# Attention heads: the swapped halves of q and k by transfers on ScalarE's queue, projections four units ahead, the output weights of the last head split earlier

## The reference

```python
def apply_rope(x, cos, sin):                       # x [B,T,H,2,64]
    x1, x2 = jnp.split(x, 2, -1)
    return jnp.concatenate([x1 * cos - x2 * sin, x2 * cos + x1 * sin], -1)

def diff_attention(...):                           # 8 heads, two maps of width 64 in each
    q, k, v = jnp.split(x @ w_in, 3, axis=-1)
    q, k = apply_rope(q, cos, sin), apply_rope(k, cos, sin)
    s = q k^T * 64 ** -0.5, causal                 # per head and map
    p = softmax(s)[map 0] - lam * softmax(s)[map 1]
    o = rms_norm(p @ v, subln_w) * (1.0 - lambda_init)
    return o @ w_out
```

## Time and profile before

| What | us |
|---|---|
| Median of 3 runs (1439.88 to 1441.41) | 1441.07 |
| The profiled execution's own time | 1440.98 |
| Its span, from first to last instruction | 1439.2 |
| TensorE busy | 1398.7 (97%) |
| VectorE busy | 868.1 (60%) |
| ScalarE busy | 649.8 (45%) |
| Attention's first `scores(0)` to its last head's | 860.18 to 1009.51 |
| Mean of the seven heads between them | 21.33 |

### The profile page before, as it was taken

The page is one execution under the profiler, slowest core; times in us unless marked ns, Lnnn a source line. Parts: engine busy times, 40 slices in busy tenths (PEclk is TensorE's granted clock), DMA queues, the critical chain, the costliest instruction groups (busy, mean ns, idle before and its releaser), DMA issues.

```text
span 1439.2 us, 20166 instructions
## 1 busy us (share of the span) xinstructions
PE 1398.7 (97%) x7042; PEld 1141.6 (79%) x7042; DVE 868.1 (60%) x1361; ACT 649.8 (45%) x1042; POOL 79.8 (6%) x92
## 2 busy tenths in 40 slices
PE   8799999999999999999999999999999999999997
PEld 7688888788788888888887876667688888888886
DVE  4566776666666666666524637777686666665226
ACT  4665666666433444444312235665524444443211
POOL 3000000000000000000001111111000000000002
PEclk9999999999999999999999999999999999999999
DMA  6122111121112333334322132121222333334331
GB/s 189 54 67 66 45 51 50 51 66 59 60 44 60 111 93 100 91 100 137 123 96 95 59 88 60 43 74 58 74 74 73 103 88 102 94 105 140 100 102 60
DMA packets 157727, 118.84 MB, mean 83 GB/s; under 512 B 5899, under 2 KB 145645, under 8 KB 157677
## 3 DMA queue, kind: packets, MB, share of 16 engines
q1 hardware_dynamic: 157676, 118.17, 27.4%
HBM read 116.04 MB, written 2.11 MB: 82 GB/s over the span
## 4 chain that ended last, share of the span: by engine, by line
PE 87%; DVE 8%; ACT 2%; issue 1%; DMA 1%; POOL 0%; SPq 0%; DVEq 0%; ACTq 0%
PE bank L1613 16%; PE bank L1615 16%; PE bank L1614 16%; PE bank L1601 8%; PE bank L1603 8%; PE bank L1602 8%; PE bank L1672 3%; PE bank L1679 2%; PE bank L1987 1%; PE bank L2005 1%; PE bank L1670 1%; PE bank L1948 1%; DVE w_lo L361 1%; PE bank L1579 1%; DVE Tc L1137 1%
## 5 line engine op out<-in xcount | busy, mean ns | idle before, releaser
L1613 PE MATMUL bank<-x_hi,w_hi 128*128 128x512 f32 (+1 forms) x1160 | 459.8, 396 | 3.6 <-DVE x_lo L1026 2.6
L1615 PE MATMUL bank<-x_hi,w_lo 128*128 128x512 f32 (+1 forms) x1160 | 438.3, 378 | 0.0
L1614 PE MATMUL bank<-x_lo,w_hi 128*128 128x512 f32 (+1 forms) x1160 | 437.7, 377 | 0.0
L361 DVE TENSOR_TENSOR w_lo<-raw,w_hi 128x1024 fp32r<-128x1024 f32 x194 | 237.9, 1229 | 243.8 <-ACT w_hi L356 238.4
L356 ACT ACTIVATE w_hi<-raw 128x1024 fp32r<-128x1024 f32 x186 | 195.0, 1051 | 168.9 <-PE bank L1603 139.6
L1613 PEld LDWEIGHTS bank<-x_hi,w_hi 128*128 128x128 f32 x1160 | 219.6, 189 | 42.0 <-issue 4.2
L1615 PEld LDWEIGHTS bank<-x_hi,w_lo 128*128 128x128 f32 x1160 | 218.9, 189 | 41.1
L1614 PEld LDWEIGHTS bank<-x_lo,w_hi 128*128 128x128 f32 x1160 | 219.7, 189 | 36.1 <-issue 2.9
L1601 PE MATMUL bank<-w_hi,u_hi 128*128 128x512 f32 x416 | 164.8, 396 | 3.0 <-DVE w_lo L361 3.0
L1603 PE MATMUL bank<-w_hi,u_lo 128*128 128x512 f32 x416 | 162.5, 391 | 0.0
L1602 PE MATMUL bank<-w_lo,u_hi 128*128 128x512 f32 x416 | 162.4, 390 | 0.0
(11 more groups left out here) (292 smaller groups left out, 1787.3 us busy)
## 6 DMA issues: line engine op xcount, KB each, us to landing
raw<-in_ffn_w_up SPq DMA_DIRECT2D x88, 512.0 KB, 3.8
raw<-in_ffn_w_down SPq DMA_DIRECT2D x44, 512.0 KB, 3.2
raw<-in_gdn_w_in SPq DMA_DIRECT2D x32, 512.0 KB, 4.1
raw<-in_diff_w_in SPq DMA_DIRECT2D x24, 512.0 KB, 3.7
raw<-in_gdn_w_out SPq DMA_DIRECT2D x8, 512.0 KB, 3.4
raw<-in_diff_w_out SPq DMA_DIRECT2D x8, 512.0 KB, 3.3
x_tok<-in_x SPq DMA_DIRECT2D x4, 512.0 KB, 5.9
ROW<-decay_rows SPq DMA_DIRECT2D x8, 256.0 KB, 3.1
```

The costliest lines, as they stand in the source:

```text
L361: nc.vector.tensor_tensor(w_lo[:, s, :], raw[:, (base + r) % RAW, :], w_hi[:, s, :].bitcast(F32), ALU.subtract).then_inc(lo_ready, 1)
L1613: nc.tensor.matmul(out, hi, x_hi[:, k, cols], start=(k == 0), stop=False)
L1614: nc.tensor.matmul(out, hi, x_lo[:, k, cols], start=False, stop=False)
L1615: ins = nc.tensor.matmul(out, lo, x_hi[:, k, cols], start=False, stop=last)
```

## The change

`rotate` is gone from TensorE. `take` on ScalarE, behind its copy, waits for that copy and for the earlier reader of the target, and then issues four transfers from `qk_raw` to a new tile `qk_rot`, each of 32 rows of 2 KB, so that the halves of each map change places. The sign that `swap` had given is now a column `turn_sign`, summed once from `swap` by VectorE, and `rope2` is made from `qk_rot`, `turn_sign` and sin by one instruction that takes both factors. VectorE waits on `rot_loaded` in place of `rot_pe`.

TensorE projects four units ahead (`AHEAD`): head h runs units 4 to 15 of head h+1 and 0 to 3 of head h+2; a head begins with `scores(0)` at once. `rope(h+1, 1)` moves on VectorE from the start of head h+1 to the end of head h, behind "oc". `take(h+1, 1)` moves on ScalarE ahead of `split_hi(2r+5)`. Four pieces of the output projection move from the last head into the head before it, and the splits of the last chunks move one place each. The hardware loop runs over four heads; the last three are written out.

```diff
-ATT_FILL = [(0, 0, 0, 0), (1, 0, 0, 1), (2, 0, 1, 0), (3, 0, 1, 1), (5, 0, 0, 2), (6, 0, 1, 2), (7, 0, 0, 3),
+ATT_FILL = [(-4, 0, 0, 0), (-3, 0, 0, 1), (-2, 0, 1, 0), (-1, 0, 1, 1), (1, 0, 0, 2), (2, 0, 1, 2), (5, 0, 0, 3),
...
+AHEAD = 4
...
             def take(g, kind):
...
                     act.wait_ge(rope_pool, 2 * g + kind - 1)
+                    act.wait_ge(rot_loaded[kind], 64 * g)
                 nc.scalar.activation(qk_raw[kind][:, :], bank[kind][:, :], ACT.Copy,
                                      scale=(HD ** -0.5 if kind == 0 else 1.0)).then_inc(bank_read[kind], 1)
+                wait_read(act, kind, T_QK // 2 + g)
+                act.wait_ge(rope_head, R_DVE0 - RD_N + RD_N * g + RD["rope2 " + "qk"[kind]])
+                for b in range(4):
+                    to, src = b * P // 4, (b ^ 1) * P // 4
+                    nc.scalar.dma_start(qk_rot[kind][to:to + P // 4, :],
+                                        qk_raw[kind][src:src + P // 4, :]).then_inc(rot_loaded[kind], 16)
...
+                dve.wait_ge(rot_loaded[kind], 64 * g + 64)
+                nc.vector.scalar_tensor_tensor(rope2[kind][:, :], qk_rot[kind][:, :], turn_sign[:, 0:1], sin[:, :],
+                                               ALU.mult, ALU.mult).then_inc(rope_head, 1)
...
-                rope(h, 1)
+                maxima(0)
...
-                if not more:
-                    hold_lo(dve, C_ATT_OUT + 6)
+                if more:
+                    rope(h + 1, 1)
+                if isinstance(h, int) and h == HEADS - 2:
+                    split_lo(dve, C_QK, it, 2 * r + 6)
...
                 def fill(p0, p1):
+                    u0, u1 = p0 + AHEAD, p1 + AHEAD
+                    if not last:
+                        project_qk(h + 1, (r + 1) % 2, u0, min(u1, 2 * KT))
+                        if not (isinstance(h, int) and h == HEADS - 2):
+                            project_qk(h + 2, r % 2, max(u0 - 2 * KT, 0), u1 - 2 * KT)
+                    shift = 0 if last else 2 * KT
+                    if isinstance(h, int) and h >= HEADS - 2:
+                        for tb, half, k in [piece for p, *piece in ATT_FILL if p0 <= p + shift < p1]:
...
-                fill(0, 1)
-                rotate(h, 1)
-                fill(1, 3)
                 pe.wait_ge(rope_head, R_DVE0 + RD_N * h + RD["kr"])
                 scores(0)
                 scores(1)
-                fill(3, 4)
+                fill(0, 4)
```

More of the change, by code:

```diff
@@ L245, in build @@
         rope2 = [place("uh", 4 + i, f"rope2{i}", [P, T]) for i in range(2)]
+        qk_rot = [place("uh", 7 + 3 * i, f"qk_rot{i}", [P, T]) for i in range(2)]
         qr = place("uh", 6, "qr", [P, T])
@@ L959, in step @@
                     out_hi(h - 1)
+                if not more:
+                    split_hi(act, C_QK, it, 2 * r + 5)
                 turned_p(0)
                 exps(1)
-                split_hi(act, C_QK, it, 2 * r + 4)
-                if not more:
-                    split_hi(act, C_QK, it, 2 * r + 5)
+                if more:
+                    split_hi(act, C_QK, it, 2 * r + 4)
+                else:
+                    hold_hi(act, C_ATT_OUT + 4, (v_head, HEADS))
                 turned_p(1)
@@ L999, in _ @@
             step(0, 0)
-            with act.Fori(0, PAIRS - 1) as it:
+            with act.Fori(0, PAIRS - 2) as it:
                 for r in (1, 2):
                     step(it, r)
-            step(0, HEADS - 1)
+            for h in range(HEADS - 3, HEADS):
+                step(0, h)
             out_hi(HEADS - 1)
@@ L1532, in step @@
                 mix(1)
-                maxima(2)
-                split_lo(dve, C_QK, it, 2 * r + 4)
                 if not more:
                     split_lo(dve, C_QK, it, 2 * r + 5)
+                maxima(2)
+                if more:
+                    split_lo(dve, C_QK, it, 2 * r + 4)
+                else:
+                    hold_lo(dve, C_ATT_OUT + 4)
                 maxima(3)
@@ L1556, in _ @@
             rope(0, 0)
+            rope(0, 1)
             split_lo(dve, C_QK, 0, 3)
             step(0, 0)
-            with dve.Fori(0, PAIRS - 1) as it:
+            with dve.Fori(0, PAIRS - 2) as it:
                 for r in (1, 2):
                     step(it, r)
-            step(0, HEADS - 1)
+            for h in range(HEADS - 3, HEADS):
+                step(0, h)
             row_factor(HEADS - 1)
@@ L1970, in fill @@
                 def fill(p0, p1):
-                    if last:
-                        for tb, half, k in [piece for p, *piece in ATT_FILL if p0 <= p < p1]:
+                    u0, u1 = p0 + AHEAD, p1 + AHEAD
[6 more added lines that the diff above has]
+                        for tb, half, k in [piece for p, *piece in ATT_FILL if p0 <= p + shift < p1]:
                             if (tb, k) == (0, 0):
@@ L1977, in fill @@
                             mixer_unit(1, tb, k, (half,))
-                    else:
-                        project_qk(h + 1, (r + 1) % 2, p0, p1)
                 def scores(qb):
@@ L2034, in step @@
                 values(2)
-                if not last:
-                    rotate(h + 1, 0)
                 turn(3)
```

39 lines of the change are left out of this document (17 added, 22 removed), and 6 rows, old and new, of the table ATT_FILL.

## The result

The changed kernel takes 1478.89 us (median of 4 runs, 1474.78 to 1480.55), the kernel before 1441.24 (4 runs, 1439.88 to 1444.42). The ratio is 1.0247, with a 95% interval of 1.0227 to 1.0267. I had said 1448, range 1437 to 1457. The direction is right; the time lies 22 us above the range.

A forecast was written before the change was run, and what follows sets the result against it. TensorE, busy 97%, bounded the kernel before; after the change it would wait for VectorE's queue each head. First head -0.1, seven heads +7.6, last head 0: +7.5 on 1441 gives 1448 us, range 1437 to 1457.

The forecast's parts named there:

- D: Time of four transfer issues in a row on ScalarE's queue, ahead of split_hi: 1.4 us, bounds 0.1 and 2.3.
- q's take with its D: cost 0, bound 0.2: In the loop, q's issues on ScalarE delay block 3's exponentials, whose mix still ends just ahead of turn(3): no cost.
- k done at 14.3, the serial sum of 4.8 on VectorE: TensorE finishes k 14.3 us after scores(0); VectorE's steps behind split_hi up to k's rope take 4.8 us.
- Landing hidden: Transfers of k land in 2.1 us behind VectorE's split, q's rope and "oc": cost 0, upper bound 0.4 a head.
- Seven heads, +7.6: Seven heads before the last take 156.95 us against 149.33: 21.95, five of 22.3, and 23.5 for head 6.
- Head 6, wait of 2.9 for chunk 1's low part: In head 6, TensorE waits 2.9 us at position 13 for the head's last split_lo, which ends at 18.7.
- Last head 0: Last head unchanged in length: waits 4.0 us in place of 3.3, one projection unit of 0.7 fewer.
- Sooner: Last head's weight splits and pieces made earlier: moves TensorE's wait for a low part (3.02 us before), doesn't end it.
- Rival 3: TensorE's clock falls in every head after its idle time: +8.4 us for seven times more, 1457; 13%.
- Rival 1: Issues on ScalarE are cheap: with D = 0.1 the kernel takes 1438.5 us, with 0.4, 1441; 20%.
- Rival 2: TensorE stays the bound because VectorE or ScalarE has slack: each head saves 2.3 us, kernel 1425; 5%.
- 1.9 + D: TensorE's new wait at the end of each head, 20.9 + D for the chain against 19.0 of its own work.

The follow-up runs named there:

- sync_issue: Changed kernel with the same four transfers a take issued by SyncE between its weight loads, none by ScalarE: 1450.73 us, ratio 1.0049 to the kernel before.
- keep_busy: Changed kernel plus unread products in each head, 12 ahead of TensorE's wait for kr and 6 ahead of values(3): 1469.58 us, ratio 1.0191.
- q_by_sync_busy: keep_busy with q's four transfers a head issued by SyncE, k's four still by ScalarE: 1465.45 us, ratio 1.0159.
- one_issue: Changed kernel with one transfer of all 128 rows per take instead of four of 32 (halves not exchanged): 1457.25 us, ratio 1.0090.
- by_product: Changed kernel with the rotation done by TensorE's product again, no transfers, all other moves kept: 1455.30 us, ratio 1.0084.
- sync_best2: Changed kernel, transfers on SyncE, three units ahead of scores(0), last heads' weights sooner, chunk 2's load before last head's turns, its pieces behind scores(1): 1428.81 us, ratio 0.9904.
- late_only: Changed kernel, transfers still on ScalarE, only scores(0) put back behind three projection units: 1465.48 us, ratio 1.0152.
- by_product_late: by_product with three projection units ahead of the wait for kr and scores(0), as in the kernel before: 1445.12 us, ratio 1.0015.
- transfers_alone: Kernel before, its order kept, with four transfers on ScalarE's queue in place of the rotation product: 1494.64 us, ratio 1.0357.

## Why the prediction was wrong

The way of k through a head can be laid beside the runs, since each run takes away one part of it. Heads at the full clock: the third to fifth of each of the middle runs, and the fourth and sixth of sync_issue. The second head is left out everywhere; it is 0.2 to 0.4 longer, with a short wait of TensorE in it. The sixth is written out behind the loop, and its way to the take is 0.2 to 0.4 shorter in the middle runs too.

| from `scores(0)` | predicted | four on ScalarE (keep_busy) | k's alone (q_by_sync_busy) | none (sync_issue) |
|---|---|---|---|---|
| to the take of k | 14.35 | 15.15 to 15.29 | 14.50 to 14.62 | 14.30 and 14.63 |
| from there to the next | 6.55 + D, with D 1.4 | 9.48 | 9.47 | 6.66 and 6.74 |
| head | 22.3 | 24.6 to 24.8 | 24.0 to 24.1 | 20.96 and 21.37 |

- **"D = 1.4": wrong, and the step that failed first.** Measured, the four are 2.45 and ScalarE is held 2.66; the head grows by 9.48 - 6.74 = 2.7. That exceeds even the high bound of 2.3. The rows I took it from the earlier trace rows were real, but of transfers to and from DRAM of 4 and 22 KB; these go from SBUF to SBUF. The nearest row by its name was not near, and the bound should have been open upwards. Here +1.3 a head. The Trainium skill's sentence on issuing ("DMA: Bandwidth & Descriptors", section "Issuing engines are not separate DMA queues"), that its time is usually small beside the transfer, helps little here: one issue is 0.61 beside a landing of 2.4 (median), a quarter, and four in a row take 2.45, as long as one landing. What it says besides the traces bear out: issued by another engine, the same transfers land much alike (2.0 in sync_issue), and what is saved is the issuer's time.
- **"q's take with its D: cost 0, bound 0.2": wrong.** exps(3) stand behind q's issues, and their mix and turn behind them; the take of k comes 0.7 later. keep_busy against q_by_sync_busy: 4.1 us in the kernel. In one_issue the head at the full clock has the take of k at 14.61, as with none: a hold of one issue, 0.5, was hidden. So the step would have stood with a small D and fell with the true one.
- **k done at 14.3, the serial sum of 4.8 on VectorE: right.** In sync_issue the take comes at 14.30 and 14.63, and 6.66 and 6.74 follow where I had 6.55. The head with no issue is 20.96 to 21.37, against 20.9. This is the mechanism of the forecast, and it stands.
- **Landing hidden: right in the loop, wrong in the first head.** The only wait of VectorE for a transfer is one of 2.8 in the first head (ScalarE's copy of k, VectorE's `rope` of k):

```profile
855.52 0.60 ACT L940 ACTIVATE qk_raw<-bank 128x512 f32<-128x512 f32 x1 [1.06 <-PE bank L1637]
861.15 0.75 DVE L1478 SCALAR_TENSOR_TENSOR rope<-qk_rot,turn_sign,sin 128x512 f32<-128x512 f32 x1 [2.76 <-DMA qk_rot<-qk_raw]
```

In the first head I had -0.1 and it was +2.6. Of the 2.7 between them, 0.8 is there before any transfer: q's copy starts at 850.14 instead of 849.35, and k's follows 5.4 later in both kernels. The last of k's four issues starts 2.46 after its copy's start instead of 1.69, which is 0.8, and it lands 3.15 after its own start where I had 2.1, which is 1.1. The loop's bound of 0.4 had a slip in it: VectorE comes to k's `rope` at 20.8 by the forecast's own sum, not at 19.4, where D was left out. So the bound was nothing at all, and the forecast is the same.
- **Seven heads, +7.6: +34.8.** Of the 27.2 too few, 7.7 net are the clock (176.49 in keep_busy against 184.16). In the 19.5 that are left, heads 1 to 5 have 11.9 (24.7 each instead of 22.3: D 1.3, q's issues 0.7, small ones 0.4), head 0 has 1.8, and head 6 has 5.8; of this last, part is keep_busy's own, whose idle products stand behind the wait for `w_lo`, since the head takes 27.22 without them.
- **Head 6, wait of 2.9 for chunk 1's low part: right**, 3.53. The low part comes at 20.3 where I had 18.7, 1.3 of it by D, and TensorE is there at 16.8 instead of 15.8.
- **Last head 0: right**; all behind the last head's `scores(0)` is +0.6. Its waits are 3.6 where I had 4.0, and a slow stretch came in head 6 and another in the last head. "Sooner" did move the wait and not end it: 3.0 before, 5.7 in two after.
- **Rival 3, the clock, 13%: came true beside the forecast**, at 9.3 us where I had priced 8.4. I had treated it as a case apart, although its own sum had waits of 2.6 in every head, and the clock fell after shorter ones in some heads (1.4 in by_product, 2.0 in sync_issue). The two should have been added. The Trainium skill ("TensorE: Matmul & The Clock Gate", section "A second HAM failure mode: psum-queue depth-cycling") tells of another kernel, in which TensorE was idle for very short whiles between groups of products, often enough for its clock to go up and down. This trace shows the like, with longer waits on other engines: heads of 0.87 to 1.00 in turn, with waits of 1.4 to 2.2 and of 2.7 in the first five.
- **Rival 1, cheap issues: false** by the issue rows. **Rival 2, TensorE the bound at 1425:** false for this kernel, but it is nearly what sync_best2 reaches, once the issues are on SyncE, `scores(0)` is late and the last heads' weights are reordered.

A condition stood in the text that I read too lightly: `scores(0)` first in a head. I counted its wait, 1.9 + D, and took it as a price of the transfers. The 1.9 is none: sync_issue has it without an issue on ScalarE. late_only and by_product_late, each 10 to 13 us faster than its pair, show that three projection units were taken from a place where they covered the chain to `kr`, to a place where they cover little: TensorE's waits for Pm are 2.9 in all in the changed kernel and 3.2 in late_only, where the units are gone from there.

Not settled: why the clock falls after one idle stretch and not after another like it. It stayed full after 2.75 at 917.04 and had fallen after 2.68 at 889.00; in by_product it fell after waits of 1.4, and in the kernel before it did not after 1.70. Where the waits were 4.1 to 4.2 in every head (transfers_alone), it fell in every head. And sync_best2's first scores come at 863.80, 3.6 later than before; 3.1 of it is there at q's first copy (852.42 against 849.35), ahead of the heads, and from 770 to 850 us its granted clock is 0.98 against 1.00. Why, no run shows.

## What to carry to other kernels

An operation taken off the busiest engine is paid for by the engine that issues its substitute: count the issues, price them from a row of the same kind of transfer (here 0.6 us each), and give them to a queue on which nobody waits. When a kernel's order is changed together with that, ask of each filler what it covered where it was. And where a forecast has the main engine idle regularly, add the fall of its clock to the sum instead of keeping it as a case of its own.

## What the runs showed of the hardware

- The issue of a transfer within SBUF takes 0.61 us (32 rows, 64 KB) on ScalarE's queue and 0.59 on SyncE's, and 0.47 with all 128 rows in one (256 KB): the count of issues sets the price, not the bytes. Two or three of a trace's 64 took 1.0 to 1.8, in three traces none.
- These transfers of 64 KB landed in 2.0 to 2.4 us (medians of the traces) beside the weights' loads, 4.0 at most, whichever of the two engines issued them.
- Eighteen products without use in each head made a kernel about 9 us faster; the granted clock stayed at 1.00 in six of seven heads, where it had been 0.87 to 0.94 in five.
- The granted clock fell to 0.93 in heads whose longest wait of TensorE was 1.4 us (by_product), and stayed at 1.00 in two heads that began after waits of 2.75 and 2.76 (the changed kernel).
